# Expert layer: the first prompt tile handled by indexed row fetches instead of dense products

## The reference

```python
def block(xb):                                   # 128 tokens
    q = (xb @ wq).reshape(PEER_BLOCK, PEER_HEADS, 2, PEER_HALF)
    s = jnp.einsum('thpd,hpkd->thpk', q, subkeys)         # 8 heads x 2 x 128 keys
    s_top, i_top = lax.top_k(s, PEER_TOPK)                # 16 of 128, twice
    cand = s_top[:, :, 0, :, None] + s_top[:, :, 1, None, :]
    g_s, g_i = lax.top_k(cand, PEER_TOPK)                 # 16 of 256 pairs
    e = jnp.take_along_axis(cand_idx, g_i, axis=-1)       # expert = 128 * key_i + key_j
    g = jax.nn.softmax(g_s, axis=-1)
    act = jax.nn.gelu(jnp.einsum('thed,td->the', u[e], xb))
    return jnp.einsum('the,thed->td', g * act, v[e])
y = layer_norm(ALPHA * h + peer(h), ln3_g, ln3_b)
```

## Time and profile before

| | |
|---|---|
| time, median of 3 | 2687.77 us |
| profiled execution, time / span | 2689.53 / 2687.8 us |
| mean granted TensorE clock | 0.938 of 2.4 GHz |
| PE / DVE / ACT / POOL busy | 91 / 61 / 26 / 19 % |
| stage_scores | 951 to 1115.5 us |
| stage_activate | 1115.5 to 1953.4 us |
| stage_experts and the layer norms | 1953.4 to 2687.8 us |

### The profile page before, as it was taken

How to read it: one execution, slowest core, us unless ns; L and a number is a source line. 1 busy time by engine, 2 the same in 40 slices (tenths; PEclk the granted TensorE clock), 3 DMA queues, 4 the chain that set the end, 5 groups by cost and what they waited for, 6 DMA issues and landing times. The chain is left out here.

```text
span 2687.8 us, 33666 instructions
## 1 busy us (share of the span) xinstructions
PE 2443.3 (91%) x11444; PEld 1882.8 (70%) x11444; DVE 1652.4 (61%) x3635; ACT 703.9 (26%) x1071; POOL 523.4 (19%) x471
## 2 busy tenths in 40 slices
PE   8998966778877689699999999999989999999997
PEld 7764843344355478588878878888868888888885
DVE  3552029592401359589879969958266666666666
ACT  1330111232001211243444444344411221211211
POOL 1000433121000000234334333433311111111110
PEclk9998987688986889899999999999989999999999
DMA  5422549567041022144555546455586666666661
GB/s 179 81 67 87 153 156 340 185 229 268 1 150 53 0 87 86 70 150 151 160 158 171 160 138 188 154 158 171 177 301 236 242 249 235 252 239 251 238 235 49
DMA packets 223200, 447.24 MB, mean 166 GB/s; under 512 B 17966, under 2 KB 105695, under 8 KB 217690
## 3 DMA queue, kind: packets, MB, share of 16 engines
q1 hardware_dynamic: 114970, 304.28, 33.9%
q10 hardware_dynamic: 84224, 67.12, 7.9%
q0 software_dynamic: 23872, 74.16, 7.5%
HBM read 368.07 MB, written 76.80 MB: 166 GB/s over the span
## 5 line engine op out<-in xcount | busy, mean ns | idle before, releaser
L2234 PE MATMUL psum<-hH,uH 128*128 128x512 f32 x1024 | 409.7, 400 | 21.4 <-PEq L1918 21.4
L2445 PE MATMUL psum<-vH,wH 128*128 128x512 f32 x1024 | 400.4, 391 | 14.8 <-DVE vL L2398 14.8
L2122 POOL TENSOR_TENSOR uL<-u_raw,uH 128x1024 fp32r<-128x1024 f32 x125 | 309.5, 2476 | 525.7 <-ACT uH L2132 525.7
L2445 PE MATMUL psum<-vH,wL 128*128 128x512 f32 x1024 | 400.0, 391 | 0.0
L2234 PE MATMUL psum<-hH,uL 128*128 128x512 f32 x1024 | 400.0, 391 | 0.0
L2445 PE MATMUL psum<-vL,wH 128*128 128x512 f32 x1024 | 399.8, 390 | 0.0
L2234 PE MATMUL psum<-hL,uH 128*128 128x512 f32 x1024 | 399.6, 390 | 0.0
L2204 DVE TENSOR_SCALAR hot_j<-iota,slots 128x128 f32<-128x128 f32 x512 | 242.3, 535 | 0.0
L2234 PEld LDWEIGHTS psum<-hH,uH 128*128 128x128 f32 x1024 | 193.2, 189 | 57.8 <-issue 21.7
L2445 PEld LDWEIGHTS psum<-vH,wH 128*128 128x128 f32 x1024 | 193.3, 189 | 56.2 <-issue 16.0
L2445 PEld LDWEIGHTS psum<-vL,wH 128*128 128x128 f32 x1024 | 193.2, 189 | 40.3
(11 more groups left out here) (419 smaller groups left out, 3304.3 us busy)
## 6 DMA issues: line engine op xcount, KB each, us to landing
u_raw<-in_uT SPq DMA_DIRECT2D x128, 512.0 KB, 3.6
activation_table<-acts ACTq DMA_DIRECT2D x128, 256.0 KB, 3.1
gate_table<-Gtile ACTq DMA_DIRECT2D x16, 2048.0 KB, 10.8
S<-in_v_rows SPq DMA_DIRECT2D x64, 512.0 KB, 9.4
v_rest<-in_v_rows SPq DMA_DIRECT2D x64, 512.0 KB, 3.5
S<-gate_table SPq DMA_DIRECT2D x16, 1024.0 KB, 7.4
S<-activation_table SPq DMA_DIRECT2D x16, 1024.0 KB, 12.3
G_rest<-gate_table SPq DMA_DIRECT2D x16, 1024.0 KB
```

The costliest lines, as they stand in the source:

```text
L2122: nc.gpsimd.tensor_tensor(uL[:, n % RU], u[:, n % RU], uH[:, n % RU].bitcast(F32), ALU.subtract).then_inc(u_split, 1)
L2234: ins = nc.tensor.matmul(bank[n % 2], w[:, n % RU, d], x[:, d, 0:SEQ], start=m == 0, stop=m == len(parts) - 1)
L2445: ins = nc.tensor.matmul(bank[2 * t + q], w[:, j, t * P:(t + 1) * P], x[:, j, q * 512:(q + 1) * 512], start=n == 0 and m == 0, stop=n == N ...
```

## The change

1. Tile 0 of the prompt leaves the dense path. Its 16,384 (token, expert) pairs lie as 128 columns, one token per partition; with the sample's 32 columns there are 160. For each column POOL fetches 128 rows of u (512 KB) in `stage_activate`, DVE makes the dot product with h (`dot`, 160 of them, spread over the steps by `STEP_DOTS`); in `stage_experts` POOL fetches 128 rows of v and DVE adds weight x row to `y_first` or `y_sample` (`add`, five per group).
2. The dense products cover three tiles: a column is 24 products of 384 tokens, a key 18 products of 512; units are 96 instead of 128; activation and gate tables are three quarters as large.
3. Routing: `stage_scores` does seven heads of tile 0, seven of tile 1 and a packed half of the sample's heads (four heads' 32 tokens in the 128 partitions, so two routings instead of eight). The index conversion runs for four heads at once, the scores are no longer copied first. Per step the numbers of columns are 1 (first pass), 5, 5 and 4.
4. `hot_j` no longer carries the gate: DVE makes both one-hots by one comparison each, and ACT multiplies `hot_j` by the gate, four instructions per unit; PE's unit waits for ACT's semaphore `gated`.
5. In `stage_experts` POOL makes `vL` of the odd keys; the weights come from the stored dots in one go; the order of the final layer norms is tiles 0, 1, sample, 2, 3.

```diff
+                for h in range(ROUTED):
+                    dve.wait_ge(s_ev, 4 * (h + 1))
+                    keys = slice(h * 2 * NKEYS, (h + 1) * 2 * NKEYS)
+                    router.head(S0[:, keys], b.first, h, c.res0)
+                    router.head(S[:, 0, keys], b.second, h, b.res)
+                    if h == BATCH - 1:
+                        router.convert(b.first, BATCH)
+                        for i in range(BATCH):
+                            router.pick(i, c.res0)
+                        router.rows_of(c.res0, 0, 64, c.ids[:, 0:NG // 2, 0:GS])
+                        router.convert(b.second, BATCH)
+                        for i in range(BATCH):
+                            router.pick(i, b.res)
+                        router.head(SS[:, 0], b.sample, 0, c.resS)
+
...
-T_COLS = (4, 4, 4, 3)
+STEP_COLS = ((1,) * 8, (5, 5, 5, 5, 5, 5, 4, 4), (5,) * 8, (4,) * 8)
+STEP_DOTS = ((2, 1) * 4, (6, 5) * 4, (6,) * 8, (6,) * 8)
...
+def gather_u(c, pool, k):
+
+    g, s = dot_at(k)
+    pool.wait_ge(c.ids_ready, 1 + min(k // 64, 2))
+    if k >= RG:
+        pool.wait_ge(c.dot_done, k - RG + 1)
+    c.nc.gpsimd.indirect_dma_start(c.ug[:, k % RG], None, c.A["u_rows"].rearrange("j i d -> (j i) d"),
+                                   bass.IndirectOffsetOnAxis(ap=c.ids[:, g, s:s + 1], axis=0)
+                                   ).then_inc(c.ug_in[k % RG], 16)
 
...
+                def dot(k):
+                    if k + 2 < NDOT:
+                        gather_u(c, pool, k + 2)
...
+                def unit(p, st, i):
+                    n = unit_of(p, st, i)
+                    act.wait_ge(slots_ready, p)
+                    act.wait_ge(hot_ready, n + 1)
+                    for q in range(UNIT):
+                        m = n * UNIT + q
+                        ins = nc.scalar.activation(hot_j[:, n % RH, q], hot_j[:, n % RH, q], ACT.Copy,
+                                                   scale=slots[:, 2, m:m + 1])
+                    ins.then_inc(gated, 1)
+                    if n:
+                        evict(n - 1)
+
...
+                def dot(k):
+                    g, s = dot_at(k)
+                    dve.wait_ge(c.ug_in[k % RG], 16 * (k // RG + 1))
+                    if k == NG * GS:
+                        dve.wait_ge(c.h_rep, 48)
+                    if k:
+                        dve.wait_ge(c.dot_done, k)
+                    V.tensor_tensor_reduce(out=prod, in0=c.ug[:, k % RG], in1=c.h[:, STILE if s == GS else 0],
+                                           scale=1.0, scalar=0.0, op0=ALU.mult, op1=ALU.add,
+                                           accum_out=c.dot[:, g, s:s + 1]).then_inc(c.dot_done, 1)
...
                         dve.wait_ge(g_mm, n - RH + 1)
-                    V.tensor_tensor(hot_i[:, n % RH], c.iota[:].unsqueeze(1).to_broadcast([P, UNIT, P]),
-                                    slots[:, 0, n * UNIT:(n + 1) * UNIT].unsqueeze(2).to_broadcast([P, UNIT, P]),
-                                    ALU.is_equal)
-                    for q in range(UNIT):
-                        m = n * UNIT + q
-                        ins = V.tensor_scalar(hot_j[:, n % RH, q], c.iota[:], slots[:, 1, m:m + 1],
-                                              slots[:, 2, m:m + 1], ALU.is_equal, ALU.mult)
+                    for q, hot in enumerate((hot_i, hot_j)):
+                        ins = V.tensor_tensor(hot[:, n % RH], c.iota[:].unsqueeze(1).to_broadcast([P, UNIT, P]),
+                                              slots[:, q, n * UNIT:(n + 1) * UNIT].unsqueeze(2).to_broadcast([P, UNIT, P]),
+                                              ALU.is_equal)
...
+                def unit(p, st, i):
+                    n = unit_of(p, st, i)
+                    pe.wait_ge(gated, n + 1)
+                    if n >= RB:
+                        pe.wait_ge(g_ev, n - RB + 1)
                     for q in range(UNIT):
-                        ins = nc.tensor.matmul(bank[2 + n % RH][:, q * P:(q + 1) * P], hot_i[:, n % RH, q],
...
+                def low_v(r, b, j):
+                    n = at(r, 2, b) * GS + j
+                    pool.wait_ge(v_hi, n + 1)
+                    pool.sem_inc(idx_seen, 1)
+                    nc.gpsimd.tensor_tensor(vL[:, j], v[j], vH[:, j].bitcast(F32),
+                                            ALU.subtract).then_inc(v_split_pool, 1)
...
-                    for dst, table, arrived in ((ug, u_table, ug_in), (vg, v_table, vg_in)):
-                        nc.gpsimd.indirect_dma_start(dst[:, p], None, table, bass.IndirectOffsetOnAxis(
-                            ap=idx[:, p:p + 1], axis=0)).then_inc(arrived[p], 16)
+                    more = r is not None or b < NG - 1
+                    if more:
+                        src = ids[:, (g + 1) * GR:(g + 2) * GR] if r is None else ids[:, bass.ds(g * GR + GR, GR)]
+                        nc.gpsimd.tensor_copy(idx[:, 1 - p], src).then_inc(idx_now, 1)
+                    low_v(r, b, 1)
+                    if more:
+                        pool.wait_ge(idx_now, g + 2)
+                        pool.wait_ge(acc0, g * GS + 3)
+                        pool.sem_inc(idx_seen, 1)
+                        for s in range(2):
+                            gather(1 - p, s)
+                    low_v(r, b, 3)
+                    if more:
+                        pool.wait_ge(acc0, g * GS + GS + 1)
...
                     V.tensor_copy(wH[:, j], wf[:, j % 2]).then_inc(d_own, 1)
-                    dve.wait_ge(d_own, n * 2 + 3)
+                    dve.wait_ge(d_own, n * 2 + 2)
                     V.tensor_tensor(wL[:, j], wf[:, j % 2], wH[:, j].bitcast(F32),
                                     ALU.subtract).then_inc(w_done, 1)
-                    dve.wait_ge(v_hi, n + 1)
-                    V.tensor_tensor(vL[:, j], v[j], vH[:, j].bitcast(F32), ALU.subtract).then_inc(v_split, 1)
+                    if j % 2 == 0:
+                        dve.wait_ge(v_hi, n + 1)
+                        V.tensor_tensor(vL[:, j], v[j], vH[:, j].bitcast(F32), ALU.subtract).then_inc(v_split, 1)
+
+                def add(r, b, s):
+                    g, p = at(r, 2, b), b % 2
+                    dve.wait_ge(vg_in[s], g * 16 + 16)
+                    dst, done, n = (y0, acc0, g * GS + (s + 1)) if s < GS else (yS, accS, g + 1)
+                    dve.wait_ge(done, n)
...
-                    dve.wait_ge(ug_in[p], at(r, 1, b // 2) * 16 + 16)
-                    V.tensor_tensor_reduce(out=prod[:], in0=ug[:, p], in1=hrep[:], scale=1.0, scalar=0.0,
-                                           op0=ALU.mult, op1=ALU.add, accum_out=dot[:, p:p + 1]
-                                           ).then_inc(dot_done, 1)
+                    add(r, b, 1)
                     prepare(r, b, 2)
+                    add(r, b, 2)
+                    add(r, b, GS)
...
-                    dve.wait_ge(gelu_done, g + 1)
-                    gate = sgate[:, g:g + 1] if r is None else sgate[:, bass.ds(g, 1)]
-                    V.tensor_tensor(sw[:, p:p + 1], sact[:, p:p + 1], gate, ALU.mult).then_inc(s_w, 1)
-                    dve.wait_ge(s_w, g + 1)
-                    dve.wait_ge(vg_in[p], at(r, 1, b // 2) * 16 + 16)
-                    dve.wait_ge(acc_done, g + 2)
-                    V.scalar_tensor_tensor(yacc[:], vg[:, p], sw[:, p:p + 1], yacc[:], ALU.mult,
-                                           ALU.add).then_inc(acc_done, 1)
-                s_w = c.sem("s_w")
+                    add(r, b, 3)
...
+                        pe.wait_ge(v_split_pool, NKEYS // 2 + 2)
+                        for t in range(STILE - 1):
                             for j in range(GS):
                                 ins = products(g * GS + j, j, t)
                             ins.then_inc(fin["tile"], 1)
+                            if t == 0:
+                                pe.wait_ge(accS, NG + 1)
+                                for q in range(2):
+                                    for m in range(4):
+                                        ins = nc.tensor.matmul(bank[6 + q][0:NS, :], c.ident[:, m * NS:(m + 1) * NS],
+                                                               yS[:, q * 512:(q + 1) * 512], start=m == 0, stop=m == 3)
+                                ins.then_inc(fin["sample"], 1)
                         return
                     for j in range(GS):
                         n = g * GS + j
                         pe.wait_ge(w_done, n + 1 + 2 * GS)
-                        pe.wait_ge(v_split, n + 1 + GS)
-                        for t in range(STILE):
...
```

More of the change, by code:

```diff
@@ L1875, in head, with convert @@
-    def head(self, scores, res, slot):
-        for part in range(4):
-            self.part(scores, res, slot, part)
+        else:
+            self.top16(res[:, 2, head * TOPK:(head + 1) * TOPK], gi[:, i], b.cand[:])
+    def head(self, x, found, head, res):
+        for part in range(3):
+            self.part(x, found, head, res, part)
```

(54 more changed lines are left out.)

447 lines of the change are left out of this document (241 added, 206 removed).

## The result

The changed kernel takes 2813.8 us (2802.7 to 2815.4, 4 runs) against 2686.8: a ratio of 1.046 [1.043, 1.049], slower. The forecast was 2617.

What follows compares the result with a forecast made beforehand. PE was taken to bound `stage_activate` and the last stage. Scores 0, `stage_activate` 0 and last stage -71 against the profiled 2689.5 gave 2618.5, less 1.8 for the median: 2617 us; range 2490 to 2710.

Steps and rivals of the forecast that it cites:

- Scores, 0: `stage_scores`: no change in time, 0 +-3 us.
- PE's side, 0.173 and 4.16: `stage_activate`: a product of 384 tokens takes 0.173 us, a column 4.16; columns and units alone 620 us.
- The new wait, 2.1 us: `stage_activate`: PE idles 2.1 us per round before its unit, waiting for ACT; bounds 1.7 to 2.6, round 7.2 us.
- Does the clock stay up?: `stage_activate`: waits of 2.1 us leave PE at 2.4 GHz, judged from idle times of 2.93 and 2.89 us.
- DVE's own load ... covered, by 4 us only: `stage_activate`, later steps: DVE's work of 29 us per step hides behind 33 us of PE's rounds.
- Rival 1: Last stage: three fetches bound the group; at a landing of 14 us, 2729 us, slower by 41; chance 0.13.
- 52 + 20.8 + 4 + 11 = 88: `stage_activate`, before the first unit: first pass 52 us, five columns 20.8, slots, one-hots and multiplications 4, PE's lateness about 11.
- The sum of the stage: `stage_activate`: first pass 52, rounds 605, fifth columns 50, first steps and DVE's lateness 106, last columns 25: 838 us.
- The blocking: A DVE instruction that meets a POOL subtraction loses about 2.1 us; last stage 2 x 2.1 us a group.
- The last stage, 19.4 and 663: DVE becomes the bound at 19.4 us per group, 621 for 32; stage 663 us, -71.
- the stall of 0.5 a group: Last stage: with a fetch landing of 10.5 us, DVE stalls 0.5 us per group.
- rival 2: Longer ACT wait (2.6 us) or DVE losing its cover (steps of 35), group 20.4 us: 2723 us; chance 0.07.

Runs made afterwards that it cites:

- edit 1: Changed kernel with ACT's multiplications of a unit's `hot_j` put ahead of the gelu of the same round: 2691.5 us, 1.002 of the kernel before.
- edit 2: Changed kernel with POOL issuing the `u` fetch of dot k+3 instead of k+2, in the same four buffers: 2778.3 us, 1.034 of the kernel before.
- edit 4: Changed kernel with the dots reading one fixed buffer, all 160 fetches still issued, fetched values left out of the sums: 2749.1 us.
- edit 13: Changed kernel with multiplications ahead of the gelu and dots reading one fixed buffer, fetched rows left out of the sums: 2544.0 us.
- edit 8: Changed kernel with DVE making all four low parts of `v` of a group in the last stage, POOL none: 2792.3 us.
- edit 7: Changed kernel with 9 idle identity products on PE before a unit's wait in all but each tile's first step: 2762.2 us.
- edit 3: Changed kernel with 18 idle identity products on PE before a unit's wait in all but each tile's first step: 2829.6 us.

## Why the prediction was wrong

- **Scores, 0:** -7 us in this trace, outside the bounds of 3. No experiment touches this stage, and in their 14 traces the next one starts between 1105 and 1117 us (median 1110), for 1108 here and 1115.5 before: a gain of some 5 us is likely, and its cause is not shown.
- **PE's side, 0.173 and 4.16:** right at 2.4 GHz.
- **The new wait, 2.1 us:** mechanism and place right, and edit 1, which only moves the multiplications, takes it away. Its size was 0.4 us short, inside the bounds of 1.7 to 2.6: from where the next product could have started it is 2.5 us (2.33 behind the pipelined end). The four multiplications took 1.28 us, not 0.88. One of them takes 0.39 us, where the row that priced them, an instruction without a factor per partition, had 0.31, and neighbours overlap by 0.09, not 0.12 (4 x 0.389 less 3 x 0.09 is 1.28). With it a round is 7.7, for 7.2: 0.5 x 84 = 42 us.

```profile
L2246 ACT ACTIVATE hot_j<-hot_j,slots 128x128 f32<-128x128 f32 x384 | 122.3, 389 | 110.5 <-DVE hot_j L2294 78.2
```

- **"Does the clock stay up?"** failed. The earlier trace rows show one idle time of 2.93 us at full clock; I carried it to a wait that returns in each round, and the sum had nothing for it. It cost some 1.6 us in 38 rounds, 60 us, and 86 us of slow products in the whole stage; filling the wait gave 52 back. The sign that the prediction had named for being wrong, a clock below 0.9 in `stage_activate`, is there (0.87).
- **"DVE's own load ... covered, by 4 us only"** failed, in that only the load was summed. Rival 1 weighed the landing of fetches in the last stage; for the 160 fetches of `stage_activate` the prediction had no wait at all. They landed in 6.4 us (4.8 to 9.4), sooner than the 9.0 of the earlier trace rows; but each is issued in POOL's order behind a low part that waits for ACT, two dots ahead. The 11 rounds of 11.9 us came from that (47 us over 7.7; edit 2 took them away), and part of the first unit's start, 117 us into the stage for 52 + 20.8 + 4 + 11 = 88: 65 us in the changed kernel (edit 4), 148 once ACT's place is mended (edit 13).
- **The sum of the stage:** 838 for 1047. The rounds are 149 us of the 209 (42 the longer wait, 60 the clock, 47 the late fetches), the time to the first unit 30. The rest, 30, lies in the first steps of later passes and in the tail, and is not taken apart.
- **The blocking** held, in both stages; edit 8 measured it: `wH` 0.50, `wL` 0.15 us each, `y_sample` 1.91, some 4.5 us a group, for 4.2 forecast. The Trainium skill's rule on it (SBUF — State Buffer, Who interferes with whom) agrees with both traces: beside GpSimd's subtractions these three are longer, without them they are not.
- **The last stage, 19.4 and 663:** right (19.35, 658), but in part by luck. Landing was 7.9, not 10.5, so the stall of 0.5 a group was not there (4 us in all 32 groups); blocking 0.3 a group above its forecast, and `wf` at 0.67 us from start to start where 0.59 was forecast (0.3 a group), made up for it. What the Trainium skill says of descriptors (SBUF — State Buffer, SBUF: two separate sides), told under rival 1, no experiment tried; in the changed kernel's trace the 95 issues of `v` fetches that overlap a cast `wH` take 1.02 us on average and the other 65 take 1.39, so it shows no issue held back by a cast.
- **Rivals:** none named the cause; rival 2 came nearest (DVE loses its cover), at 2723 and 0.07. It had 0.5 us a round where 1.8 were lost (754 - 605 over 84), as it left out the clock and the fetches. The range ended at 2710, 104 us short.

How far low clock and fetch waits overlap is not settled: slow fell with every edit that shortened a wait.

## What to carry to other kernels

When work moves to another engine, look at where it stands in that engine's order: four short multiplications behind the gelu cost 122 us; ahead of it they cost no more than 9 us over having VectorE do them. Price a fetch by issue plus landing against its lead in the issuing engine's order, and ask what that engine waits for first. A wait that returns in each round can cost its length and the clock after it.

## What the runs showed of the hardware

PE kept 2.4 GHz through one idle time of 2.93 us, but in `stage_activate`, where 2.33 us of idleness returned every 7.7 to 9.2 us, it fell to 1.2 GHz again and again (38 of 84 rounds at 9.1 to 9.9 us for 7.7); nine identity products in each wait held the clock at 0.98. At a DMA share of 1.00 (376 GB/s) an indexed fetch of 128 rows landed in 7.7 us (median), no later than at 0.91 (7.9). Nine identity products of 128 columns of f32 took 2.17 us (edit 7), eighteen 4.18 us (edit 3). Four multiplications of 128 x 128 by a factor per partition took 1.28 us on ACT.
